# Attention stage of a three-block layer kernel: the projection of a block is read out in the next block, one Silu pass per head, and the exponentials go behind the work that frees accumulator banks

## The reference

```python
ATTN_HEADS = 8                    # two query/key maps of width 64 per head, values of width 128
def diff_attention(q, k, v, lam, slopes):
    """q, k (b,s,h,2,d); v (b,s,h,e); lam scalar; slopes (h,).
    out_t = sum_s [softmax1 - lam*softmax2]_{ts} v_s, both maps with ALiBi."""
```

## Time and profile before

| | |
|---|---|
| median of three timed runs | 4264.54 us |
| the profiled execution's own time | 4258.0 us |
| its span in the profile | 4256.2 us |
| TensorE busy | 3781.0 us, 89% of the span |
| VectorE busy | 2176.0 us, 51% |
| ScalarE busy | 1661.1 us, 39% |
| granted TensorE clock, mean | 0.954 |

### The profile page before, as it was taken

One profiled execution on the slowest core, in us unless ns is written; L12 is line 12 of the kernel. 1 busy time (PEld: TensorE's weight loads), 2 busy tenths in 40 slices (PEclk: granted clock), 3 DMA queues, 4 the chain that ended last, 5 costly groups with the idle time before them and its releaser, 6 DMA issues.

```text
span 4256.2 us, 48874 instructions
## 1 busy us (share of the span) xinstructions
PE 3781.0 (89%) x20470; PEld 3138.8 (74%) x20470; DVE 2176.0 (51%) x2835; ACT 1661.1 (39%) x2243; POOL 527.9 (12%) x437
## 2 busy tenths in 40 slices
PE   6989999999988999888888876999888898879998
PEld 5768978778766777666666655988777777768988
DVE  3444243343464666445545452367777777743222
ACT  4323122212134556455565562134444544431122
POOL 0000010000000535100000000012222222210002
PEclk9989999999998999999999997999999999999999
DMA  2102111111111010100100004121111111143101
GB/s 88 30 26 80 31 65 50 50 40 50 50 41 60 26 44 11 45 23 25 29 26 25 25 28 153 41 80 40 40 40 40 35 40 45 40 160 127 40 30 65
DMA packets 196398, 211.31 MB, mean 50 GB/s; under 512 B 7943, under 2 KB 171732, under 8 KB 196180
## 3 DMA queue, kind: packets, MB, share of 16 engines
q1 hardware_dynamic: 190420, 187.22, 13.8%
q10 hardware_dynamic: 5760, 20.97, 1.3%
HBM read 174.62 MB, written 33.55 MB: 49 GB/s over the span
## 4 chain that ended last, share of the span: by engine, by line
PE 66%; DVE 17%; ACT 10%; issue 5%; DMA 1%; POOL 0%; SPq 0%; ACTq 0%; DVEq 0%; POOLq 0%
PE pd L211 56%; PE pq L211 7%; DVE t L2461 2%; ACT t L2392 2%; ACT t L311 2%; DVE t L2762 2%; DVE t L320 1%; PE pd L359 1%; PE pq L359 1%; DVE t L2479 1%; DVE t L3165 1%; DVE t L2754 1%; DVE t L1793 1%; DVE t L3150 0%; ACT L2373 0%
## 5 line engine op out<-in xcount | busy, mean ns | idle before, releaser
L211 PE MATMUL pd<-t 128*128 128x512 f32 (+2 forms) x15920 | 3107.9, 356 | 117.5 <-DVE t L607 34.9
L211 PEld LDWEIGHTS pd<-t 128*128 128x128 f32 x15920 | 2573.4, 192 | 603.8 <-issue 154.0
L211 PE MATMUL pq<-t 128*128 128x128 f32 (+5 forms) x3222 | 571.0, 341 | 105.0 <-ACT t L2806 19.3
L211 PEld LDWEIGHTS pq<-t 128*128 128x128 f32 (+2 forms) x3222 | 404.2, 187 | 217.0 <-issue 50.3
L311 ACT ACTIVATE t<-t 128x2048 fp32r<-128x2048 f32 (+2 forms) x150 | 245.2, 1635 | 761.0 <-PE pd L211 670.3
L320 DVE TENSOR_TENSOR t<-t 128x2048 fp32r<-128x2048 f32 (+2 forms) x150 | 298.0, 1988 | 307.4 <-ACT t L311 306.9
L359 PE MATMUL pd<-t 128*128 128x128 f32 x800 | 128.8, 307 | 160.2 <-ACT t L2373 62.3
L359 PEld LDWEIGHTS pd<-t 128*128 128x128 f32 x800 | 106.8, 158 | 184.0 <-ACT t L2373 65.9
L1393 DVE TENSOR_TENSOR t<-pd,t 128x512 f32<-128x512 f32 x256 | 171.7, 689 | 122.8 <-PE pd L211 122.8
L2503 DVE COPY t<-pd 128x512 f32<-128x512 f32 x64 | 44.2, 690 | 269.5 <-PE pd L359 269.4
L2392 ACT ACTIVATE t<-t 128x1024 f32<-128x1024 f32 x128 | 146.0, 1142 | 87.9 <-DVE t L2466 87.9
(11 more groups left out here) (290 smaller groups left out, 2820.9 us busy)
## 6 DMA issues: line engine op xcount, KB each, us to landing
t<-in_w_in_dram SPq DMA_DIRECT2D x97, 512.0 KB, 4.0
t<-in_w_mlp_dram SPq DMA_DIRECT2D x32, 1024.0 KB, 5.4
t<-in_w_out_dram SPq DMA_DIRECT2D x20, 1024.0 KB, 5.1
t<-in_w_in_dram SPq DMA_DIRECT2D x16, 1024.0 KB, 5.3
t<-ym_scratch ACTq DMA_DIRECT2D x24, 512.0 KB, 7.7
t<-in_x_dram SPq DMA_DIRECT2D x16, 512.0 KB, 7.6
x_scratch<-t SPq DMA_DIRECT2D x16, 512.0 KB, 2.9
ym_scratch<-t SPq DMA_DIRECT2D x16, 512.0 KB, 2.6
```

What stands on the lines that cost most here:

```text
L211: ins = e.matmul(out, l, r, start=(first and j == 0), stop=(last and j == n - 1), skip_group_check=True)
```

## The change

Five things are done, all in the attention stage:

- ScalarE and VectorE read out the projection of block n - 1 in block n (n from 1 to 56), where they read that of block n at its end.
- On ScalarE, the projection's read-out, the unit's split, the copy of the transposed values and the Ln and Exp of the mean square stand ahead of the exponentials of block n + 2; only `act_att_values` and the copy of `wT` stand behind them.
- On VectorE, the projection's read-out stands behind the maxima of block n + 2 and ahead of the copy of `wT`.
- The first half of g is copied raw to SBUF; the Silu of the second half is followed by a Silu of the first half in place.
- TensorE's, GpSimd's and SyncE's programs keep their order.

```diff
@@ act_att_out, kind g
-            e.activation(gT[:, sl], b[:, :], ACT.Silu).then_inc(*at.inc("act", "agt", h, th, free=("ag", h, th)))
+            if th == 0:
+                e.copy(gT[:, sl], b[:, :]).then_inc(*at.inc("act", "agr", h, free=("ag", h, th)))
+            else:
+                e.activation(gT[:, sl], b[:, :], ACT.Silu).then_inc(*at.inc("act", "agt", h, 1, free=("ag", h, th)))
+                e.wait_ge(*at["agr", h])
+                e.activation(gT[:, half(0)], gT[:, half(0)], ACT.Silu).then_inc(*at.inc("act", "agt", h, 0))
@@ act_stage_att
             if n + 1 < BLOCKS:
                 scaled(n + 1)
+            if 0 < n < 57:
+                act_att_out(e, (n - 1) // NT + 1, KIND[tt - 1], (tt - 1) % 2)
+            if h < 7 and tt % 2 == 0:
+                if (h, tt) == (6, 6):
+                    e.wait_ge(*at["scores", 6, 7, 1])
+                act_unit(e)
+            if tt >= 6 and h < 7:
+                act_att_vt(e, h + 1, tt - 6)
+            act_att_ms(e, *owed(n))
             if n + 2 < BLOCKS:
                 scores(n + 2)
             if tt % 4 == 0 and n:
                 act_att_values(e, n - 4)
-            if tt >= 6 and h < 7:
-                act_att_vt(e, h + 1, tt - 6)
-            act_att_ms(e, *owed(n))
             e.wait_ge(*at["wT", n, 0])
             e.copy(WT[:, 0:4, tile(tt % 4)], four(PD.of("wT", n, 0)[:, :])).then_inc(
                 *at.inc("act", "wTc", n, 0, free=("wT", n, 0)))
-            if h < 7:
-                act_att_out(e, h + 1, KIND[tt], tt % 2)
-                if tt % 2 == 0:
-                    if (h, tt) == (6, 6):
-                        e.wait_ge(*at["scores", 6, 7, 1])
-                    act_unit(e)
@@ dve_stage_att
                 scores(n + 2)
+            if 0 < n < 57:
+                dve_att_out(e, (n - 1) // NT + 1, KIND[tt - 1], (tt - 1) % 2)
             e.wait_ge(*at["wT", n, 1])
...
-            if h < 7:
-                dve_att_out(e, h + 1, KIND[tt], tt % 2)
-                if tt % 2 == 0:
-                    dve_unit(e)
+            if h < 7 and tt % 2 == 0:
+                dve_unit(e)
```

## The result

The changed kernel takes 4119.73 us (median of 4 runs, 4118.38 to 4121.18), the kernel before, run beside it, 4263.65 us: the ratio is 0.9664, with a 95% interval of 0.9647 to 0.9681. The forecast was 4128 us, range 4112 to 4168, faster. The profiled execution takes 4119.16 us, with a span of 4117.3; the forecast for it was 4122.

The account below looks back on a forecast made before the run. TensorE was taken as the bound, with a floor of 82.2 us in head 3's 102.2; gains of 16.4 (head 0), 95 (1 to 5), 20.9 (6) and 4 (7), together 136, gave 4128 us against 4264.5, range 4112 to 4168.

Parts of the forecast that it names:

- TensorE as the bound, and its floor: Attention stage: TensorE is nearest to full, and its work without stops takes 82.2 us of head 3's 102.2.
- The laid-out head: One head written out by hand in the new order: 83.0 us, of which 0.8 is stops; 83.2 taken.
- The sum: Gains over the heads: 16.4 us in head 0, 95 in heads 1 to 5, 20.9 in 6, 4 in 7; together 136.
- The median: Median of the runs put 6.5 us above the profiled execution, so 4122 became 4128 us.
- The slow clock: TensorE's slow clock behind stops, 1.6 us in block 0 and 1.0 in block 3, goes; granted clock of 0.99.
- The Silu: One Silu load and one reload fewer per head, 2.6 us, one 0.6 us copy more; costed at nothing by itself.
- The moved stops: Rival: ScalarE's lateness keeps the waits for wT's copy and the maxima, plus half the slow clock; 4162 us, chance 0.14.
- Slower by the projection's bank: Rival: banks 0 and 1, freed one block later, make TensorE wait ahead of each projection; 4280 us, chance 0.03.
- The drain after a table load: Rival: the Ln ends 1.4 us later, so block 2 stops for 1.5 us instead of 0.1; 4138 us, chance 0.02.
- The weights: Rival: a late weight transfer holds the unit's split, now ahead of the exponentials; no gain, chance 0.01.

Follow-up runs that it names:

- the run with 1.1 us more per block: Changed kernel with four small copies added on ScalarE ahead of the exponentials in each of the 56 blocks with a projection: 4148.29 us.
- the bank order alone: Kernel before, with only ScalarE's copy of the transposed values and mean square moved ahead of the exponentials: 4207.12 us.
- eight copies in block 5: Changed kernel with eight small copies added on ScalarE ahead of the exponentials, only in block tt = 5, 7 blocks: 4140.68 us.

## Why the prediction was right

- *TensorE as the bound, and its floor.* 82.2 us a head were worked out; 82.3 to 82.4 us of busy time were measured, and the plain block stayed at 8.2 us.
- *The laid-out head.* 83.0 us, against 83.1. The blocks 0 to 7 began at 0, 15.1, 23.3, 32.6, 40.8, 55.9, 65.1, 74.4 by hand; by the profile of head 3 at 0, 15.1, 23.2, 32.5, 40.7, 55.8, 64.8, 74.4. The stop in block 6 was put at 0.7 and is 0.96 us; the one at the Ln of block 2 was put at 0.1 and is 0.2 us. ScalarE is where it was put, too: its copies of wT in blocks 1 and 2 end at 24.8 and 36.7 us, laid out were 24.9 and 36.8. So the agreement is not only one of sums.
- *The sum.* Heads 0 to 6: 132.3 us forecast, 133.6 measured. Head 7: 4 forecast, which was a choice between bounds, 6.3 measured; putting the mean square back behind the exponentials takes 5.5 of it away. Together 136 against 139.9.
- *The median.* The 6.5 us by which the earlier median stood above the profiled execution were carried over to the changed kernel, where the two differ by 0.6. This is 5.9 of the 8.3 us between 4128 and 4119.7; it was a choice without a row behind it.
- *The slow clock.* It was said to go with the stops, and heads 1 to 6 have a granted clock of 1.00. The sign named for the stage, 0.99, was missed by a little: its mean is 0.98, by heads 0 and 7.
- *The Silu: the step that was wrong.* "I cost it at nothing by itself; the cover is AV." Undone alone it is worth 11.7 us. The 14 table loads fewer came as said (61 before, 47 after). The sum was right all the same because the head was laid out with the single pass in it; the words beside it gave the gain to the other parts. The cover was named wrongly: the copy of wT of block 7 comes before AV, not beside it.
- *The moved stops.* The rival left 17.1 + 7.4 us of waits for the copy of wT and the maxima in place; 5.1 + 1.9 are left. But its mechanism is real: the run with 1.1 us more per block shows it at work, at 26.7 us, and the bank order alone shows it too. The slacks were as thin as the rival said, and the forecast rested on them.
- *Slower by the projection's bank.* No wait of TensorE ahead of a projection shows in heads 1 to 6, and 1.1 us more per block brought none in heads 0 to 6 either. Lateness of 7.5 us, where it would decide, was not tried.
- *The drain after a table load.* Not there: the Ln starts 0.01 us behind the end of its load in block 5 of the changed kernel (2104.84 + 1.28, then 2106.13), as in the earlier trace rows. The Trainium skill, "ScalarE: Activation LUTs", section "What ACT_TABLE_LOAD costs", gives a drain of about 1380 ns with each switch. The trace does not agree: with it the stop at the Ln of block 2 would be 1.5 us, and it is 0.2.
- *The weights.* They cost nothing; no wait of TensorE names them.

## What to carry to other kernels

An engine with 40% idle time can still be what stops the busiest one, by the order of its work: put ahead what frees a buffer that is wanted in this block, and let what is wanted only in the next block be late. Such a change can be costed by writing out one period (here a head) by hand, from durations in the trace, with the time at which each buffer is wanted beside the time at which it comes free. And work is covered only by what runs after the thing that it delays; ask which product waits for the delayed result before naming a cover.

## What the hardware showed that was not expected

The same stop can cost the clock or not. With eight copies in block 5, a stop of 3.12 us left the granted clock of that block at 1.00 and one of 3.09 us at 0.87, with the 24 products behind it taking 5.72 and 7.34 us. With the mean square behind, two equal blocks of 11.52 us (waits of 2.23 and 2.24 us) were followed by a block at 1.00 and one at 0.83, 8.19 and 9.79 us. With four copies in every block even a wait of 1.85 us was followed by 24 products in 7.33 us, in a block with a granted clock of 0.86, where after 1.83 us they took 5.73. The clock has the two levels of 1.2 and 2.4 GHz, and in these three pairs the dip costs 1.6 us each. What decides whether a stop is followed by a dip was not found.
